# Latent attention with finer waits and moved sums; a pooled mixer that multiplies before it normalises

## The reference

```
# latent attention (first part): k_up, v_up from a normalised 256-wide latent, q from a normalised 384-wide one
kv = rms_norm(h @ w_in[kv], kv_norm_g) @ w_ukv ;  q = rms_norm(h @ w_in[q], q_norm_g) @ w_uq
o  = softmax(q k^T / sqrt(96)) v          # 8 heads, 64 + 32 rotated channels

# second part, layer 1
h = rmsnorm(x) * g_norm1 * (1 + scale) + shift
u = h @ w_in_odd                          # 1024 x 1024
p = centred window mean of u over tokens (windows 2, 4, 8, 16 by channel group) - u
x = x + gate * (p @ w_grp) * s_pool
# both layers of the second part end with
x = x + gate2 * moe(modulate(rmsnorm(x)), router, 16 experts, 32 tokens each, 1024 -> 1024 -> 1024)
```

## Time and profile before

| | us |
|---|---|
| median of 3 executions | 1810.87 (1810.51 to 1811.75) |
| profiled execution, its time | 1813.82 |
| its span, first to last instruction | 1811.7 |
| PE busy | 1552.6 |
| DVE busy | 666.8 |
| ACT busy | 390.3 |

### The profile page before, as it was taken

One profiled execution on the slowest core, in us unless ns is written; L12 is line 12 of the kernel. 1 busy time (PEld: TensorE's weight loads), 2 busy tenths in 40 slices (PEclk: granted clock), 3 DMA queues, 4 the chain that ended last, 5 costly groups with the idle time before them and its releaser, 6 DMA issues.

```text
span 1811.7 us, 21729 instructions
## 1 busy us (share of the span) xinstructions
PE 1552.6 (86%) x8888; PEld 986.6 (54%) x8888; DVE 666.8 (37%) x1511; ACT 390.3 (22%) x690; POOL 46.6 (3%) x64
## 2 busy tenths in 40 slices
PE   6989999999999999998987767777799968677766
PEld 4544468878888876767442433334455424243433
DVE  3257666648898357685210101000222101010102
ACT  4222251021220024323221211111213211121111
POOL 0000000000110000001000000000000000000000
PEclk9999999999999999998998888888999988898889
DMA  9445744867549924214899999999988999999996
GB/s 365 168 165 186 266 158 151 313 252 282 207 165 342 356 95 164 94 72 198 373 429 428 429 428 429 428 429 428 410 364 350 429 429 428 429 428 429 428 428 287
DMA packets 110829, 572.52 MB, mean 316 GB/s; under 512 B 9188, under 2 KB 15460, under 8 KB 86184
## 3 DMA queue, kind: packets, MB, share of 16 engines
q1 hardware_dynamic: 109776, 569.79, 77.9%
q10 hardware_dynamic: 984, 1.79, 0.3%
HBM read 570.51 MB, written 1.05 MB: 315 GB/s over the span
## 4 chain that ended last, share of the span: by engine, by line
PE 60%; DMA 33%; DVE 3%; ACT 2%; SPq 1%; issue 1%; DVEq 0%; ACTq 0%
DMA ring<-in_w_exp_up_dram 29%; PE bank L496 18%; PE bank L1311 9%; PE bank L983 8%; PE bank L1014 4%; DMA ring<-in_w_exp_down_dram 2%; PE bank L504 2%; PE bank L1337 2%; PE bank L1391 2%; PE bank L1347 2%; PE bank L1298 2%; PE bank L1032 2%; PE bank L657 1%; DMA ring<-in_w_ada_dram 1%; PE bank L715 1%; PE bank L667 1%
## 5 line engine op out<-in xcount | busy, mean ns | idle before, releaser
L1311 PE MATMUL bank<-ring,arena 128*32 128x512 f32 x1792 | 257.0, 727 | 188.0 <-DMA ring<-in_w_exp_up_dram 185.9
L1311 PEld LDWEIGHTS bank<-ring,arena 128*32 128x32 f32 x1792 | 67.1, 130 | 374.0 <-issue 224.6
L2731 DVE COPY arena<-bank 128x256 f32<-128x256 f32 x32 | 13.6, 425 | 575.0 <-PE bank L1327 575.0
L983 PE MATMUL bank<-hT,ring 128*128 128x256 f32 x704 | 153.5, 379 | 0.0
L983 PEld LDWEIGHTS bank<-hT,ring 128*128 128x128 f32 x704 | 133.2, 190 | 20.4 <-issue 2.6
L1337 PE MATMUL bank<-ring,arena 128*32 128x512 f32 x960 | 125.0, 664 | 4.7 <-DMA ring<-in_w_exp_down_dram 2.8
L1932 ACT COPY arena<-bank 128x512 f32<-128x512 f32 x32 | 33.4, 1044 | 429.8 <-PE bank L1311 429.8
L496 PE MATMUL bank<-ring,hT 128*128 128x512 f32 (+2 forms) x320 | 124.9, 545 | 0.0
L1347 PE MATMUL bank<-arena 128*128 128x256 f32 x512 | 119.0, 385 | 1.8 <-DVE arena L2744 1.8
L1347 PEld LDWEIGHTS bank<-arena 128*128 128x128 f32 x512 | 94.6, 190 | 41.2 <-issue 29.6
L1298 PE MATMUL bank<-arena 128*128 128x32 f32 x960 | 109.9, 274 | 0.0
(11 more groups left out here) (375 smaller groups left out, 1623.0 us busy)
## 6 DMA issues: line engine op xcount, KB each, us to landing
ring<-in_w_exp_down_dram SPq DMA_DIRECT2D x60, 2048.0 KB, 19.3
ring<-in_w_exp_gate_dram SPq DMA_DIRECT2D x56, 2048.0 KB, 19.1
ring<-in_w_exp_up_dram SPq DMA_DIRECT2D x56, 2048.0 KB, 23.4
ring<-in_w_mod_dram SPq DMA_DIRECT2D x16, 2048.0 KB, 14.4
ring<-in_w_ada_dram SPq DMA_DIRECT2D x12, 2048.0 KB, 13.7
ring<-in_w_up_dram SPq DMA_DIRECT2D x10, 2048.0 KB, 13.6
ring<-in_w_in_dram SPq DMA_DIRECT2D x8, 2048.0 KB, 8.6
arena<-in_w_mod_dram SPq DMA_DIRECT2D x8, 2048.0 KB, 7.8
```

Of the source, the lines that this page charges most:

```text
L983: ins = pe.matmul(b[:, 0:T], x[:, k, j * 128:j * 128 + 128], hT[:, k, 0:T], start=(k == 0), stop=(k == KD - 1))
L1311: ins = pe.matmul(bank[0][32 * q:32 * q + 32, :], xe[:, k * CAP:(k + 1) * CAP], xs[q // 2][:, o:o + 512], start=(k == 0), stop=(k == KD - ...
```

## The change

There are two edits, in latent attention and around the pooled mixer.

Latent attention: `qct` is turned within the `kv` loop after block 2, in the second ring; instead of one wait for all `kv` evictions, the keys of heads 0 to 3 wait for half 0 and the others for half 1; two of the four `qT` banks are of the second ring; scores wait only for the `kT` and `qT` of their head. DVE and ACT divide `kT` 4 to 7 otherwise (ACT 4, 5; DVE 6, 7). The 48 sums are spread as `MLA_SUMS`: none at steps 0 and 1, then 4 and 3 in turn, 2 at the last.

The pooled mixer: `hT` gets `xT` times the gain alone, neither divided by the root nor shifted ("lifted", DVE, between the additions to `xT`); PE multiplies it at once, half 0 of the columns first for both token blocks, and the mean square of a token comes as a column (`mt7`) from POOL's sums. The product of the shift with `w_in_odd` is made by DVE (16 instructions over the weights, `shift_sum`) and two products with ones (`hw`); DVE evicts `u` as bank times the reciprocal root of the token plus this row. The table is kept as two bands of 136 columns. `router_shift(1)` goes to the start of the expert part of layer 0.

```diff
+MLA_SUMS = (0, 0) + (4, 3) * 6 + (4, 2)
+POOL_BAND, POOL_LO = 136, (0, 120)
-POOL_SUMS = (2, 3, 5, 6, 8)
+POOL_SUMS = (2, 3, 5, 6, 7, 8)
...
+                    if tag == "mla" and qb == 0:
+                        G.read(pe, ("kT", h))
+                        G.read(pe, ("qT", hp))
...
+                if tb == 2:
+                    pe.wait_ge(sem("q_norm"), 2)
+                    for j in range(3):
+                        b = G.open(pe, ("qct", j), second=True)
+                        turn(("qct", j), b, [qc[:, tk, j * 128:j * 128 + 128] for tk in range(TB)])
...
-            for tb in range(4):
-                for hf in range(2):
-                    G.read(pe, ("kv", tb, hf))
             for h in range(4):
                 b = G.open(pe, ("kT", h))
+                for tb in range(4):
+                    if h == 0:
+                        G.read(pe, ("kv", tb, 0))
...
+            for tb in range(4):
+                G.read(pe, ("kv", tb, 1))
...
-                b = G.open(pe, ("qT", hp))
+                b = G.open(pe, ("qT", hp), second=hp > 1)
...
+                if layer == 0:
+                    router_shift(1)
                 b = G.open(pe, ("aT", layer))
...
-            norm(7)
-            router_shift(1)
-            xs = [w3(weights(pe, ("o_in", g)), KD, 512) for g in range(2)]
+            xs = [w3(weights(pe, ("o_in", 0)), KD, 512)]
...
             for k in range(KD):
-                normed(7, k + 1)
+                pe.wait_ge(sem("lifted"), k + 1)
                 for tb in range(TB):
-                    for g in range(2):
...
+                    pool_in(tb, 0, k)
+            m = G.open(pe, "mt7", second=True)
+            pe.wait_ge(sem("squares"), KD * 7 + KD)
+            pe.wait_ge(sem("square_sum"), (KD - 2) * (POOL_SUMS.index(7) + 1))
...
+            xs.append(w3(weights(pe, ("o_in", 1)), KD, 512))
+            for k in range(KD):
+                pool_in(0, 1, k)
+            for g in range(2):
+                pe.wait_ge(sem("shift_summed"), g + 1)
+                b = G.open(pe, ("hw", g), second=True)
+                G.close(pe.matmul(b, ones, shift_sum[:, g, :], start=True, stop=True), ("hw", g))
+            for k in range(KD):
+                pool_in(1, 1, k)
             G.over(("o_in", 0), ("o_in", 1))
...
+                for k in range(TB):
+                    lo = POOL_LO[k]
+                    ins = pe.matmul(b[:, lo:lo + POOL_BAND], u_tm[:, k, c * 128:c * 128 + 128],
+                                    x[:, k, (c // 2) * POOL_BAND:(c // 2 + 1) * POOL_BAND],
+                                    start=(k == 0), stop=(k == 1), skip_group_check=True)
...
-                for k in range(3 * i, 3 * i + 3):
+                done_before = sum(MLA_SUMS[:i])
+                for k in range(done_before, done_before + MLA_SUMS[i]):
                     mod_sum(4 + k // KD, k % KD, k % KD + 1)
...
+                def lift(n):
+                    dve.wait_ge(sem("moe_added"), n + 1)
+                    dve.tensor_scalar(hT[:, n, 0:T], xT[:, n, :], gains(6)[:, n:n + 1], None,
+                                      ALU.mult).then_inc(sem("lifted"), 1)
...
+            for g, tb in ((0, 0), (0, 1), (1, 0), (1, 1)):
+                G.read(dve, ("hw", g))
+                b = G.take(dve, ("u", tb, g))
+                G.give(dve.scalar_tensor_tensor(u_tm[:, tb, g * 512:g * 512 + 512], b, pool_root[:, tb:tb + 1],
+                                                shift_out[:, g, :], ALU.mult, ALU.add), ("u", tb, g))
```

More of the change, by code:

```diff
@@ L576, in router_shift @@
                 pe.wait_ge(sem("routers_in"), 32)
[L577 removed]
+                b = G.open(pe, ("sW", layer))
                 by = mc(1 + layer, 3)
@@ new lines, in _ @@
+            m = G.open(pe, "mt7", second=True)
+            pe.wait_ge(sem("squares"), KD * 7 + KD)
+            pe.wait_ge(sem("square_sum"), (KD - 2) * (POOL_SUMS.index(7) + 1))
+            for row in (KD - 2, KD - 1):
+                for tb in range(TB):
+                    ins = pe.matmul(m[:, 2 * tb:2 * tb + 2], sq_late[:, row, tb * 128:tb * 128 + 128], ones[:, 0:2],
+                                    start=(row == KD - 2 and tb == 0), stop=(row == KD - 1 and tb == 1),
+                                    skip_group_check=True)
@@ L1395, in _ @@
+            G.close(ins, "mt7")
+            xs.append(w3(weights(pe, ("o_in", 1)), KD, 512))
[7 more added lines that the diff above has]
+                pool_in(1, 1, k)
             G.over(("o_in", 0), ("o_in", 1))
-            for tb in range(TB):
-                for g in range(2):
-                    G.read(pe, ("u", tb, g))
@@ L1399, in _ @@
-            x = w3(weights(pe, "pool"), TB, 4 * T)
+            x = w3(weights(pe, "pool"), TB, 4 * POOL_BAND)
             for c in range(KD):
+                if c % 4 == 0:
+                    for tb in range(TB):
+                        G.read(pe, ("u", tb, c // 4))
                 b = G.open(pe, ("p", c))
-                chain(("p", c), b[:, 0:T], lambda k: u_tm[:, k, c * 128:c * 128 + 128],
-                      lambda k: x[:, k, (c // 2) * T:(c // 2) * T + T], TB)
+                for k in range(TB):
[3 more added lines that the diff above has]
+                                    start=(k == 0), stop=(k == 1), skip_group_check=True)
+                G.close(ins, ("p", c))
@@ L1558, in squares @@
                 if c:
-                    act.wait_ge(done, G.number[("mt", 0) if c == 7 else ("ms", c - 1)])
+                    act.wait_ge(done, G.number[{7: ("mt", 0), 8: "mt7"}.get(c, ("ms", c - 1))])
                 for k in range(KD):
@@ L1954, in _ @@
             squares(7, xT, added(0))
[L1955 to L1959, removed]
+            b = G.take(act, "mt7")
+            G.give(act.activation(pool_root, b[:, 0:4].rearrange("p (b c) -> p b c", b=TB)[:, :, 0], ACT.Sqrt, bias=eps,
+                                  scale=1.0 / D), "mt7")
+            for g in range(2):
+                evict(("hw", g), shift_out[:, g, :])
             for c in range(1, KD, 2):
@@ L2749, in experts @@
                                              xT[:, n, :], ALU.mult, ALU.add).then_inc(sem("moe_added"), 1)
+                if layer == 0:
+                    lift(KD - 1)
                 dve.wait_ge(sem("moe_added"), KD * (layer + 1))
             experts(0, 6)
-            set_gain(6, mc(2, 1), vc("g_norm1_2", KD, KD))
-            link(dve.tensor_tensor(gains(0), mc(2, 2), vc("s_pool_2", 0, KD), ALU.mult))
-            norm(7, xT, gains(6), hT[:, :, 0:T])
-            for tb in range(TB):
-                evict(("u", tb, 0), u_tm[:, tb, 0:512])
+            by, xs = mc(2, 0), []
+            for g in range(2):
+                sl, count_in = place[("o_in", g)]
+                dve.wait_ge(slot_full[sl], count_in)
+                xs.append(w3(ring[:, sl * SLOT:(sl + 1) * SLOT], KD, 512))
+                for k in range(KD):
+                    if k == 0:
+                        ins = dve.tensor_scalar(shift_sum[:, g, :], xs[g][:, 0, :], by[:, 0:1], None, ALU.mult)
+                    else:
+                        ins = dve.scalar_tensor_tensor(shift_sum[:, g, :], xs[g][:, k, :], by[:, k:k + 1],
+                                                       shift_sum[:, g, :], ALU.mult, ALU.add)
+                    if k < KD - 1:
+                        link(ins)
+                ins.then_inc(sem("shift_summed"), 1)
+            G.read(dve, "mt7")
+            link(dve.reciprocal(pool_root, pool_root))
+            for g, tb in ((0, 0), (0, 1), (1, 0), (1, 1)):
[3 more added lines that the diff above has]
+                                                shift_out[:, g, :], ALU.mult, ALU.add), ("u", tb, g))
             for c in range(0, KD, 2):
```

47 lines of the change are left out of this document (26 added, 21 removed).

## The result

The changed kernel takes 1794.31 us in the median of 7 executions (1788.0 to 1801.43), against 1810.87 for the kernel before in the same rounds (7 executions, 1803.87 to 1814.97): a ratio of 0.9915, interval 0.9898 to 0.9931. The forecast was 1792.2 with a range of 1788.5 to 1798.0. 1.8 us of it stand ahead of all that was edited: latent attention's first product starts at 39.37 us instead of 41.19.

What follows compares the result with a forecast made beforehand. PE was taken to bound the kernel up to each expert layer, whose end follows the resumption of its DMA stream. Attention 7.3 plus mixer 11.9 minus router shift 0.5 gives 18.7 us: 1792.2 us, range 1788.5 to 1798.0.

Steps and rivals of the forecast that it cites:

- The room: Ahead of the second expert layer: DMA's idle time lets at most 15 us of PE savings reach the end.
- Rival F: No change: transfers ahead of `gate_up(0)` hide every edit, leaving 1810.9 us; chance 0.02.
- start of `u`: Pooled mixer: `u` follows the last scatter directly, at 1300.2 instead of 1307.23; 7.0 us gained.
- the narrower product: Pooled product on table bands of 136 columns: 3.8 us instead of 7.0, 3.2 gained.
- rival C: Pooled product no faster when narrower, since weight loading sets its pace; loses 3.2 us, 1795.4; chance 0.05.
- rival E: Slower: `hw` products wait for DVE's 16 late shift instructions and hold up PE's queue; chance 0.02.
- The clock: Full instead of half clock at `u`, 3.3 us, and at attention's first steps, 2.0 us.
- rival B: Half clock stays at `u`; loses 3.3 us, 1795.5; chance 0.09.
- rival A: Attention gains only its first part: DVE sets the pace or the clock falls; loses 4.0, 1796.2; chance 0.12.
- Attention: Latent attention: 3.3 us before the scores, 2.0 from the freed first steps, 2.0 from the clock; 7.3 in sum.
- Rival D: Attention's gain is swallowed downstream by a transfer that comes at its own time; 1799.5 us, chance 0.07.
- The router shift at layer 0: Moved shift takes 1.85 us where PE idled 1.39, before the turn of the affinities; 0.46 us lost.

Runs made afterwards that it cites:

- less `u`: Changed kernel with 12 of the 32 products of `u` left out, so that `u` is incomplete; 1791.07 us, ratio 0.9900.
- more `u`: Changed kernel with each of the two `hw` products made four times, the first three to no effect; 1797.92 us, ratio 0.9926.
- before again: The kernel before, unedited, measured and traced once more; 1812.63 us, ratio 1.0008.
- attention only: Kernel before with only the latent attention edit; pooled mixer, table and router shift as before; 1802.19 us, ratio 0.9959.
- router shift before u: Changed kernel with the router shift of layer 1 put back directly ahead of `u`; 1795.19 us, ratio 0.9918.
- pooled mixer only: Changed kernel with latent attention put back as before, the router shift staying at layer 0; 1801.0 us, ratio 0.9947.
- even sums: Changed kernel with three column sums at every attention step again, finer waits kept; 1800.13 us, ratio 0.9947.
- after again: The changed kernel, unedited, measured and traced once more; 1793.11 us, ratio 0.9915.

## Why the prediction was right, and where its sizes were off

**What bounds the kernel.** Right, and borne out by the profiles of less and more `u` and by the constant time from the resumption to the end. The room was put at 15 us, 11.9 taken and 3 left; 12.1 were taken and the traces of after left 5.0 and 6.0, of which 4.4 and 6.4 could be had. Rival F (no change) falls with the ratio.

**The pooled mixer.** From the last scatter to the output product it took 10.72 + 31.68 + 6.99 = 49.4 us and takes 3.53 + 30.08 + 3.70 = 37.3: 12.1 against 11.9 forecast. By terms: start of `u` 7.2 (7.0); the `u` products 13.73 + 6.97 + 6.87 = 27.6 instead of 30.7, 3.1 (3.3; the recorded working divides 24.2 us by 28 and writes 0.857, it is 0.864, which makes 27.7 us and 3.0); the 1.00 us before the pooled product gone (1.0); the narrower product 3.3 (3.2); `mt7` 0.8 and `hw` 1.7 (0.9, 1.7). The narrower product is 32 records in 3.71 us, 0.23 us a matmul, so rival C falls. By the estimate made from the 81 ns at 128 columns in the Trainium skill (TensorE: Matmul & The Clock Gate, Back-to-back issue gap) it would have been 5.2; the measurement decides against that here. DVE ended the second group of the shift at 1305.4 and PE asked at 1310.22: 4.8 us of cover, 4.5 forecast, so rival E had no hold.

**The clock.** Over all eleven profiles (both kernels and nine more) the places are clean. `u` ran at half clock in the four with a pause or 16-column products ahead of it (before, before again, attention only, router shift before u) and at 1.00 in the other seven; the `gk` product of step 3 was slow in the four with the 2.58 us wait (before, before again, pooled mixer only, even sums) and at 1.00 in the other seven. So rival B and the second part of rival A fall. Not every pause does it: the 1.39 us that PE still stands at step 1, which the prediction feared, and the 1.37 us ahead of `kv` left the clock at 1.00 in the 3 us behind them, in all seven profiles with the new sums. What the prediction left out is that half clock lies elsewhere too, and not always in the same place: at 210 to 218 (0.79; 1.1 us from z to w_up) in three of the seven profiles with the new sums and in none of the other four, in the router part (0.50 at 1337 to 1341, in code that did not change; its eight wide products take 5.30 us, and took 4.68 before), and at times in `gate_up(0)` of either layer. The clock was valued in the sum at 2.0 + 3.3 us, and that much was saved where it was forecast: 2.2 (1.3 in the transposes and scores of step 2, 0.9 in the `gk` product) and 3.1. Some was paid elsewhere; whether because it was saved, or by the chance of the execution, the traces can't separate. The mean granted clock of the whole span, 0.933 before and 0.934 after, doesn't tell, since most of the half clock lies where DMA sets the pace. The stage of the first expert layer behind its `gate_up(0)`, first before, then after:

```profile
880.00:1296.50 416.50, 316.02 (x2272) 160.22 (x2272) 40.73 (x120) 66.70 (x74) 0.00 (x0) 0.89 1.01 428
868.00:1285.20 417.20, 318.23 (x2275) 160.83 (x2275) 41.20 (x122) 66.70 (x74) 0.00 (x0) 0.88 1.01 428
```

Summed over both expert layers beyond their `gate_up(0)`, PE had half clock for 198 to 216 us in each of the eleven profiles, by the clock records of the traces. Where PE is the chain (kvr to the first rows of layer 0, and the last scatter to the end of `gate_up(0)` of layer 1) it had half clock for 39.8 and 39.7 us in the two profiles of before, and 26.4 and 29.8 in those of after: so less of it was left there.

**Attention.** 3.96 us to the scores (3.3; after again has it at nearly the granted clock of before, 0.82 and 0.67 against 0.83 and 0.66 at 30 to 40 and 40 to 50 us): `q` starts 2.4 us earlier (2.07 forecast), the last turns 3.2, and the scores follow them without the wait for DVE. From the scores to z 4.3 us (4.0). Even sums lose 4.7 there, so all of it belongs to the one line `MLA_SUMS`. DVE did not become the pace (busy for 68.1 of the 92 us from 98 to 190). Rival A falls. Rival D falls as well, nothing downstream swallows the gain: attention alone gives 7.4 us, 7.3 forecast.

**The router shift at layer 0.** PE's timeline there: the shift, then the turn of the affinities without a wait.

```profile
844.57 1.07 PE L511 MATMUL bank<-cst,hT 128*128 128x128 f32 x8
845.47 1.86 PE L587 MATMUL bank<-arena,modc 128*128 128x16 f32 x16
847.18 0.42 PE L511 MATMUL bank<-cst,small 128*16 128x128 f32 x2
```

From the turns to the affinities it is 2.61 us, and 2.45 in the kernel with attention only, which has no shift there: 0.2 lost, 0.46 forecast.

**The sum.** The stages that were edited gain 12.1 + 4.0 + 4.3 - 0.2 = 20.2 us, 1.5 more than the 18.7 forecast; the medians move by 16.6 and, in the second measurement, 18.1, and the ratio by 15.4 (12.5 to 18.5). So by the medians 2 to 5 us are given back outside them. Seen in both traces of after are 1.1 us from z to w_up and 0.75 us from y to the first rows; in one of them, 1.7 in `gate_up(0)`. On the other side, the stage ahead of the experts of layer 0 was 2.65 us shorter in both (222.55 against 225.20), but 225.61 and 225.64 in more and less `u`, which have the same code there, so it is not counted; an execution like those would be 3 us slower there. In three other profiles the first expert layer was 3 to 4 us longer. Parts of these sizes come and go with the granted clock in code that nobody edited. What the prediction's sum lacked is thus an entry for them; that it is the clock that takes the 2 to 5 us in the median execution is likely and not shown, and in which stage stays open: one profile for each kernel can't tell. The forecast of 18.7 us lies between the 20.2 of the edited stages and the 15.4 to 18.1 of the medians. That it comes as near to these is in part luck: its terms fell short by 1.5 us, and what is given back was not among them.

## What to carry to other kernels

Where an expert layer is bound by its stream of weights, look ahead of it for stretches in which DMA stands idle; PE time saved there reaches the end, to within 1 to 2 us in these profiles, until that gap is used up, and its length can be estimated beforehand (3 us forecast, 5.0 and 6.0 found). A serial pause of PE ahead of wide products can cost more than itself: behind the pauses of 1.88 us (with 16-column products ahead of it) and 2.58 us the clock was half in each of the profiles that had them, behind those of 1.4 us within latent attention it was not, in the seven profiles with the new sums. Moving DVE work of no urgency out of the first steps, or multiplying first and normalising at the eviction, takes both away. But do not count on the whole of such a gain in the median: half clock also turned up in stages that nobody edited.

## What the runs showed beyond that

- The mean granted clock of the profiles lies between 0.930 and 0.938 in all eleven, although `u` and the `gk` product changed between half and full clock. It is a mean over the expert layers above all (0.87 to 0.89 there in the profiles of before and after), where PE waits for DMA, and says little of the stages where PE is the chain.
- The stretch from kvr to the scores took 56.4 to 59.4 us in kernels whose code for it is the same, and in the shortest the granted clock was 1.00 where it was 0.74 at 40 to 50 us in the profile of after. Likewise the stage ahead of the experts of layer 0 (222.0 to 225.6 us) and the first expert layer (430.2 to 434.5 us). The spread of 3 to 13 us among executions of one kernel is larger than most single edits of this change; the stage lengths are what made them visible.
